# Moving the prompt's spectral product and one output gating from VectorE to GpSimd in a hybrid HGRN2 / Hyena step

## What is computed

```python
def _long_conv(u, kern):
    uf = jnp.fft.rfft(u, n=2 * L, axis=1)
    kf = jnp.fft.rfft(kern, n=2 * L, axis=0)
    return jnp.fft.irfft(uf * kf[None], n=2 * L, axis=1)[:, :L]

# _mixer
u = x1 * v
z = _long_conv(u, kern) + hy_d * u
y_hy = x2 * z
y_hy = y_hy * lax.rsqrt(jnp.mean(y_hy * y_hy, axis=-1, keepdims=True) + EPS) * hy_norm_w
merged = jnp.concatenate([o_hg, y_hy], axis=-1)
out = jnp.einsum('ble,ed->bld', merged, w_out)

# _layer
x = x + g1 * mix
```

## Time and profile before

| | us |
|---|---|
| median of 3 runs (lowest to highest) | 913.55 (912.89 to 916.66) |
| the profiled execution, its own time | 912.88 |
| its span (what the trace shows) | 911.1 |
| TensorE busy (share of the span) | 887.6 (97%) |
| VectorE busy | 717.0 (79%) |
| ScalarE busy | 443.3 (49%) |
| GpSimd busy | 38.9 (4%) |

### The profile page before, as it was taken

The page is one execution under the profiler, slowest core; times in us unless marked ns, Lnnn a source line. Parts: engine busy times, 40 slices in busy tenths (PEclk is TensorE's granted clock), DMA queues, the critical chain, the costliest instruction groups (busy, mean ns, idle before and its releaser), DMA issues.

```text
span 911.1 us, 14075 instructions
## 1 busy us (share of the span) xinstructions
PE 887.6 (97%) x5374; PEld 788.7 (87%) x5374; DVE 717.0 (79%) x911; ACT 443.3 (49%) x710; POOL 38.9 (4%) x58
## 2 busy tenths in 40 slices
PE   7999999999999999999899999999999999999997
PEld 4479898898898898688779999999999999998885
DVE  5744755966966985699678899999999999988645
ACT  5745324334343323332276756556565656565443
POOL 2200000100000000002000000000000000000000
PEclk9999999999999999999999999999999999999999
DMA  8765233144134244325511232233313232345703
GB/s 297 244 217 174 83 126 138 37 157 145 63 122 145 91 164 137 89 70 112 144 46 48 76 131 99 97 110 114 115 62 130 108 111 88 131 152 202 261 0 116
DMA packets 39275, 112.76 MB, mean 124 GB/s; under 512 B 4471, under 2 KB 12663, under 8 KB 38568
## 3 DMA queue, kind: packets, MB, share of 16 engines
q1 hardware_dynamic: 33944, 93.58, 30.3%
q0 software_dynamic: 4800, 17.99, 6.5%
q10 hardware_dynamic: 464, 0.30, 0.1%
HBM read 101.48 MB, written 10.37 MB: 123 GB/s over the span
## 4 chain that ended last, share of the span: by engine, by line
PE 84%; DVE 9%; ACT 3%; issue 2%; DMA 1%; ACTq 0%; DVEq 0%; POOLq 0%
PE ps L2005 19%; PE ps L2006 19%; PE ps L2007 19%; PE ps L2505 14%; PE ps L2226 4%; PE ps L2025 2%; PE ps L2086 2%; PE ps L2238 1%; PE ps L2363 1%; DMA part<-in_rates 1%; DVE w_lo L1377 1%; PE ps L2033 1%; PE ps L2246 1%; DMA w<-in_hy_w 1%; ACT xn L1154 1%
## 5 line engine op out<-in xcount | busy, mean ns | idle before, releaser
L2005 PE MATMUL ps<-h_hi,w_hi 128*128 128x320 f32 x620 | 196.3, 317 | 2.8 <-DVE w_lo L1377 1.4
L2007 PE MATMUL ps<-h_hi,w_lo 128*128 128x320 f32 x620 | 191.6, 309 | 0.0
L2006 PE MATMUL ps<-h_lo,w_hi 128*128 128x320 f32 x620 | 191.5, 309 | 0.0
L2005 PEld LDWEIGHTS ps<-h_hi,w_hi 128*128 128x128 f32 x620 | 116.6, 188 | 4.1 <-issue 3.1
L2006 PEld LDWEIGHTS ps<-h_lo,w_hi 128*128 128x128 f32 x620 | 116.6, 188 | 0.0
L2007 PEld LDWEIGHTS ps<-h_hi,w_lo 128*128 128x128 f32 x620 | 116.4, 188 | 0.0
L1868 DVE TENSOR_TENSOR w_lo<-raw,w_hi 128x1024 fp32r<-128x1024 f32 (+1 forms) x53 | 64.2, 1212 | 18.6 <-ACT w_hi L1220 17.6
L1220 ACT ACTIVATE w_hi<-raw 128x1024 fp32r<-128x1024 f32 (+1 forms) x53 | 55.5, 1047 | 31.8 <-PE ps L2007 31.7
L1377 DVE TENSOR_TENSOR w_lo<-raw,w_hi 128x1024 fp32r<-128x1024 f32 x44 | 53.4, 1224 | 6.4 <-ACT w_hi L904 5.2
L2005 PE MATMUL ps<-w_hi,h_hi 128*128 128x512 f32 x120 | 49.6, 413 | 2.0 <-DVE h_lo L1734 2.0
L904 ACT ACTIVATE w_hi<-raw 128x1024 fp32r<-128x1024 f32 x44 | 45.8, 1057 | 4.4 <-DMA raw<-in_slots 2.4
(11 more groups left out here) (320 smaller groups left out, 2067.2 us busy)
## 6 DMA issues: line engine op xcount, KB each, us to landing
raw<-in_slots SPq DMA_DIRECT2D x138, 512.0 KB, 4.7
acts<-actf POOLq DMA_DIRECT2D x22, 320.0 KB, 2.5
raw<-in_slots SPq DMA_DIRECT2D x24, 256.0 KB, 6.5
xf<-acts SPq DMA_DIRECT2D x12, 320.0 KB, 6.6
wsum<-acts SPq DMA_DIRECT2D x10, 320.0 KB, 7.7
xin<-in_x_sample SPq DMA_DIRECT2D x4, 512.0 KB, 11.2
grow<-gates POOLq DMA_DIRECT2D x2, 1024.0 KB, 12.3
x<-in_x_sample POOLq DMA_DIRECT2D x2, 1024.0 KB, 13.7
```

What stands on the lines that cost most here:

```text
L2005: mm(out, lhs[0], rhs[0], start=first, stop=False)
L2006: mm(out, lhs[0], rhs[1], start=False, stop=False)
L2007: return mm(out, lhs[1], rhs[0], start=False, stop=last)
```

## The change

GpSimd takes over two pieces of VectorE's work. The prompt's spectral product becomes seven instructions on GpSimd, linked to each other, behind `up_ready`; their scratch tiles are now `sq` and `x1[:, 1, NT - 1, :]` in place of `prod`, and the last one raises a new semaphore, `up_multiplied`. The gating becomes ten GpSimd instructions of 128x512, one for each tile, each behind its own `raw_taken`. VectorE's `gate_raw` and its product are gone. ScalarE's copy of the tenth tile waits for `up_multiplied`, since that tile's place is scratch until then, and TensorE's `z_prompt(0)` waits for it too. The other edits give several semaphores of the kernel's first part one shared name (`silu_in` and `bound_in` become `exp_in`, and so on) with the counts adapted, and move VectorE's wait for `ld_gate1` to before `mix_tile`.

```diff
@@ gpsimd @@
+            eng.wait_ge(sem("up_ready"), 1)
+            r, t = sq[:, 0:HW], x1[:, 1, NT - 1, :]
+            G = nc.gpsimd.tensor_tensor
+            link(G(r, Up[:, 0, :], kspec_p[:, 0, :], ALU.mult))
+            link(G(t, Up[:, 1, :], kspec_p[:, 1, :], ALU.mult))
+            link(G(r, r, t, ALU.subtract))
+            link(G(t, Up[:, 0, :], kspec_p[:, 1, :], ALU.mult))
+            link(G(Up[:, 1, :], Up[:, 1, :], kspec_p[:, 0, :], ALU.mult))
+            link(G(Up[:, 1, :], Up[:, 1, :], t, ALU.add))
+            link(nc.gpsimd.tensor_copy(Up[:, 0, :], r), "up_multiplied")
+
+            eng.wait_ge(sem("ld_gate1"), 16)
             for n in range(2):
                 cols = slice(n * HW, (n + 1) * HW)
-                eng.wait_ge(sem("raw_gated"), n + 1)
+                for i in range(NT):
+                    eng.wait_ge(sem("raw_taken"), n * NT + i + 1)
+                    x = x1[:, n, i, :]
+                    nc.gpsimd.tensor_tensor(x, x, grow1[:, int(i == NT - 1), cols], ALU.mult).then_inc(sem("raw_gated"), 1)
+                eng.wait_ge(sem("raw_gated"), (n + 1) * NT)
...
-            eng.wait_ge(sem("zspec_ready"), 3)
+            eng.wait_ge(sem("zspec_ready"), 2)
             load(grow2[:, :, :], gates[1].partition_broadcast(P), "ld_gate2")
@@ scalar @@
             for n in range(2):
                 for i in range(NT):
                     eng.wait_ge(sem("hg_mixed"), n * NT + i + 1)
+                    if n * NT + i == 2 * NT - 1:
+                        eng.wait_ge(sem("up_multiplied"), 1)
                     A(x1[:, n, i, :], ps[:, HG_BANKS[(n * NT + i) % 2], :], ACT.Copy).then_inc(sem("raw_taken"), 1)
@@ vector @@
             multiply(0)
             multiply(1)
-            eng.wait_ge(sem("up_ready"), 1)
-            r, t = prod[:, 0, 0, :], prod[:, 1, 0, :]
-            link(V.tensor_tensor(r, Up[:, 0, :], kspec_p[:, 0, :], ALU.mult))
...
-            link(V.tensor_copy(Up[:, 0, :], r), "zspec_ready")
-            def gate_raw(n):
...
-            eng.wait_ge(sem("ld_gate1"), 16)
-            gate_raw(0)
             for k in range(2):
                 split_lo(UNIT_WOUT + 4 + k)
-            gate_raw(1)
```

More of the change, by code:

```diff
@@ L813, in store_state @@
                 load(io["new_state"][0, 0].rearrange("d h k w -> h k d w")[h], newst[:, :, :], "state_stored")
+            link = linker(eng, "pool_own")
             def gate_out(which):
@@ L828, in _ @@
             eng.wait_ge(sem("raw_in0"), 32)
-            load(ktab[:, :, :, :, :], io["ktab"], "ld_ktab")
-            load(ptab_k[:, :, :], io["ptab"][:, 0], "ld_ktab")
+            load(ktab[:, :, :, :, :], io["ktab"], "filter_dma")
+            load(ptab_k[:, :, :], io["ptab"][:, 0], "filter_dma")
             def first_row(n):
@@ L837, in first_row @@
                 eng.wait_ge(sem("taps_ready"), n + 1)
-                nc.gpsimd.tensor_tensor(forth, forth, back, ALU.add).then_inc(sem("first_sum"), 1)
-                eng.wait_ge(sem("first_sum"), 1 + n // 4)
+                link(nc.gpsimd.tensor_tensor(forth, forth, back, ALU.add))
                 nc.gpsimd.tensor_copy(back, forth).then_inc(sem("first_row"), 1)
@@ L864, in _ @@
             eng.wait_ge(sem("head_steps"), HEADS * STEPS)
-            load(ptab[:, :, :, :], io["ptab"][:, 1:3], "ld_ptab")
+            load(ptab[:, :, :, :], io["ptab"][:, 1:3], "spectra_dma")
             gate_out(1)
@@ L951, in _ @@
             eng.wait_ge(sem("ld_vec"), 16)
-            eng.wait_ge(sem("silu_in"), 1)
-            A(gate_c, gate_c, ACT.Exp).then_inc(sem("silu_exp"), 1)
+            eng.wait_ge(sem("exp_in"), 1)
+            A(gate_c, gate_c, ACT.Exp).then_inc(sem("exp_done"), 1)
             eng.wait_ge(sem("ld_rates"), 16)
@@ L959, in _ @@
                   bias=rates[:, bias:bias + 1]).then_inc(sem("decay_ready"), 1)
-            eng.wait_ge(sem("bound_in"), 1)
-            A(bound[:, 1, :], bound[:, 0, :], ACT.Exp).then_inc(sem("bound_exp"), 1)
+            eng.wait_ge(sem("exp_in"), 2)
+            A(bound[:, 1, :], bound[:, 0, :], ACT.Exp).then_inc(sem("exp_done"), 1)
             A(stat[:, 2, 0, 0:1], eps[:, :], ACT.Sqrt)
@@ L1415, in _ @@
                     link(V.tensor_scalar(fr, fr, 0.5 / math.pi, None, ALU.mult))
-                eng.wait_ge(sem("hid_made"), i + 1)
+                eng.wait_ge(sem("filter_made"), i + 1)
                 if i:
@@ L1427, in _ @@
             eng.wait_ge(sem("ld_vec"), 16)
-            link(V.tensor_scalar(gate_c, v("c", 0, 2 * KD), -1.0, 80.0, ALU.mult, ALU.min), "silu_in")
+            link(V.tensor_scalar(gate_c, v("c", 0, 2 * KD), -1.0, 80.0, ALU.mult, ALU.min), "exp_in")
             lb = v("lb_f", 0, 2 * NC)
-            link(V.tensor_tensor(bound[:, 0, :], lb, lb, ALU.subtract), "bound_in")
+            link(V.tensor_tensor(bound[:, 0, :], lb, lb, ALU.subtract), "exp_in")
             def sum_groups(e):
@@ L1462, in damp @@
                 eng.wait_ge(sem("decay_ready"), n + 1)
-                eng.wait_ge(sem("taps_made"), n + 1)
+                eng.wait_ge(sem("filter_made"), n + 3)
                 b = tap_banks(n)
@@ L1493, in join @@
                 link(V.tensor_tensor(kspec[:, m, 1, cs, :], first, second, ALU.subtract), "kspec_ready")
-            eng.wait_ge(sem("silu_exp"), 1)
+            eng.wait_ge(sem("exp_done"), 1)
             link(V.tensor_scalar(gate_c, gate_c, 1.0, None, ALU.add))
@@ L1508, in _ @@
             join(0)
-            eng.wait_ge(sem("bound_exp"), 1)
+            eng.wait_ge(sem("exp_done"), 2)
             link(V.reciprocal(bound[:, 2, :], bound[:, 1, :]))
@@ L2049, in tap_pair @@
                         if d:
-                            last.then_inc(sem("taps_made"), 1)
+                            last.then_inc(sem("filter_made"), 1)
             def tap_prompt():
@@ L2109, in _ @@
             mm(ps[0:NHID, 0, 0:SIDE], w1[0:NEMB, :], feats[0:NEMB, 0:SIDE], start=True, stop=True)
-            mm(ps[NHID:P, 0, 0:SIDE], w1[0:NEMB, :], feats[0:NEMB, SIDE:2 * SIDE], start=True, stop=True).then_inc(sem("hid_made"), 1)
+            mm(ps[NHID:P, 0, 0:SIDE], w1[0:NEMB, :], feats[0:NEMB, SIDE:2 * SIDE], start=True, stop=True).then_inc(sem("filter_made"), 1)
             keep_busy(4)
@@ L2115, in _ @@
                 last = mm(ps[rows, 0, 0:SIDE], w2[rows, :], hid[rows, 0, :], start=True, stop=True)
-            last.then_inc(sem("hid_made"), 1)
+            last.then_inc(sem("filter_made"), 1)
             keep_busy(4)
@@ L2128, in _ @@
             ada_turn(0)
-            eng.wait_ge(sem("ld_ktab"), 32)
+            eng.wait_ge(sem("filter_dma"), 32)
             filter_dft(0)
@@ L2366, in _ @@
             eng.wait_ge(sem("uspec_ready"), 1)
-            eng.wait_ge(sem("ld_ptab"), 16)
+            eng.wait_ge(sem("spectra_dma"), 16)
             for cs in range(2):
```

## The result

The changed kernel is slower: 928.22 us median of 4 runs (927.26 to 929.67), against 914.25 us before (912.89 to 916.66, 4 runs). The ratio is 1.0151, with a 95% interval of 1.0124 to 1.0179. The forecast was 926.7 us. The profiled execution of the change took 929.67 us, its slowest, and has a span of 927.9 us.

The account below looks back on a forecast made before the run. The chain of waits was taken to bound the kernel, TensorE holding 84%, VectorE 9%. A 13.1 us TensorE wait and 1.8 us of clock start the loop over `c` 13.8 us later: 912.9 + 13.8 = 926.7 us, range 916 to 932.

Parts of the forecast that it names:

- The bound of the gain: At VectorE's loop over `c`: it can start no earlier than `z_ready` allows, so at most 1.1 us of 10.9 is gained.
- strict turns: Beside VectorE's `multiply` calls: GpSimd and VectorE alternate at their shared port, ending `multiply(1)` 17.3 us later; chance 0.60.
- Starving: Rival: VectorE's next instruction always gets in first, GpSimd finishes late, `mix_tile(0)` waits for a DMA; 919 to 921 us, chance 0.17.
- Cheap hand-over: Rival: GpSimd holds the port only partly, below 0.25 us delay each, so TensorE never waits; 911.8 us, chance 0.10.
- Some turns only: Rival: GpSimd gets in at every second chance, VectorE loses eight to ten turns; 918 to 920 us, chance 0.10.
- The hold of one instruction: Beside `multiply`: each GpSimd TENSOR_TENSOR delays VectorE by about 1.05 us, the COPY by 0.46 us.
- the sum: `multiply(1)` 17.3 us later less 4.2 us cover gives TensorE a 13.1 us wait; the loop over `c` starts 13.8 us later.
- The clock: At TensorE's inverse transforms after its wait: some 3.5 us at half speed, adding 1.8 us.
- From the loop to the end: Behind the loop over `c`: norm and FFN follow in one chain, so its 13.8 us shift reaches the end.
- The two new waits cost nothing: ScalarE's tenth copy and TensorE's `z_prompt(0)` wait for a product done near 398.1 undisturbed, with 17 us of cover.

Follow-up runs that it names:

- e5: The changed kernel with all seventeen GpSimd instructions, semaphores and waits kept, but on 32 of 512 columns; 913.03 us, ratio 0.9993 to before.
- e8: The changed kernel with the ten GpSimd gatings replaced by copies of a tile onto itself; 922.91 us, ratio 1.0087 to before.
- e7: The changed kernel with all four residual DMAs issued behind the tenth gating instead of two in the middle; 927.67 us, ratio 1.0148 to before.
- e9: The changed kernel with 62 filling matmuls on TensorE ahead of its wait for the latent products; 927.78 us, ratio 1.0153 to before.
- e3: The changed kernel with GpSimd's gating held back until VectorE has finished the latent products; 925.63 us, ratio 1.0130 to before.
- e6: The changed kernel with 52 filling matmuls on TensorE ahead of its wait for the latent products; 930.13 us, ratio 1.0175 to before.
- e2: The changed kernel with the prompt's product back on VectorE, gating alone on GpSimd, ScalarE's new wait gone; 921.89 us, ratio 1.0091 to before.
- e1: The changed kernel with the gating back on VectorE, the prompt's product alone on GpSimd; 915.79 us, ratio 1.0032 to before.

## Why the prediction was right, point by point

- **The bound of the gain** (1.1 us, set by `z_ready`) was right: 1.09 us in e5.
- **The mechanism** was right: strict turns between GpSimd's instructions and VectorE's with two SBUF inputs. The doubled products in the change show it, and the dose in e5, e8 and the change. The rule of the exclusive lock in the Trainium skill (SBUF — State Buffer, section "SBUF: two separate sides") agrees with these runs in the main: in e5 a 32-column GpSimd instruction waits out a VectorE product (1185 ns in all). Its "for the whole instruction" doesn't fit the measured hold, which was 0.98 of GpSimd's 1.28 us; and the product that five gatings kept out, one after the other, goes beyond what that rule would give.
- **Starving** fell: VectorE was delayed from the first turn on, and `mix_tile(0)` waited for no DMA. **Cheap hand-over** fell: 0.98 us per instruction against the 0.25 us at which it would decide. **Some turns only** fell: every product beside GpSimd's work gave a turn, until the long hold, where GpSimd got five in a row.
- **The hold of one instruction** was 0.98 us and not 1.05, and the COPY's 0.29 and not 0.46. Sixteen and one make 16.0 us, where I had 17.3; e7, which has these turns and nothing else, has 15.9 (`multiply(1)` ends 38.79 us behind the spectrum copy instead of 22.88).
- **What the sum did not have** is the product held through five gatings. It brings the delay of `multiply(1)` from 15.9 to 18.65 us (five turns would have cost 4.9 us, the hold cost 7.5). So TensorE's wait was 14.4 to 14.6 us and not 13.1.
- **The clock** was 2.28 us in the transforms and not 1.8: the low level lasted about 4.4 us of work after the wait, and not 3.5. e9 agrees with 2.04 us at the loop. It is no fixed price: behind waits of 2.06 to 14.42 us the first two transforms took 1.7 to 3.1 us longer, and not in the order of the waits, and in e3 0.1 us.
- **From the loop to the end** I carried the shift through unchanged. It lost 1.67 us on the way, as the second dip of the clock moved. At the loop the shift was 15.76 us against 13.8 forecast, and only with this loss does it come to 14.09 at `mix_tile(0)`. That the total is so near (926.7 us against a median of 928.22, 14.0 us over before) is in part luck: a turn that I had too large, a hold and a clock that I had too small, and a dip that moved nearly cancel.
- **The two new waits cost nothing**, as said: ScalarE's tenth copy began at 418.21 right behind its matmuls, and the product was done at 406.95.
- The limit of the evidence: that each turn is decided per instruction comes from the lockstep of the two timelines. No kernel here took VectorE's two-input instructions away while GpSimd worked at the same place; that PSUM inputs keep VectorE free is shown only by the rows of before.

## What to carry to other kernels

Before moving work from VectorE to an idle GpSimd, look at what VectorE runs at that moment: beside instructions with two inputs in the on-chip memory, most of the moved work's time is paid for by VectorE (0.98 of 1.28 us here), wherever in its critical stretch it falls. Here that is more than VectorE saves: it did such a 128x512 product itself in 0.69 us. Look also for a short instruction of one engine that took several times its usual duration somewhere in the trace; one such row, 0.70 us instead of 0.166, carried this forecast. And ask first what the freed engine would wait for next: of 10.9 us taken off VectorE, 1.1 us were ever to be had.

## What the runs showed that was not expected

- Behind two DMA issues from GpSimd, followed by unlinked gatings, one VectorE instruction took 8.70 us in the change (8.84 in e6, 8.88 in e9), 7.37 us in e3 and 4.92 us in e2, and with copies in place of the gatings 2.72 us (e8). With linked gatings it was 4.11 us, and without the DMA issues in between there was no such hold (e7). Why the DMA issues bring it about stays open. In the change the product started at 417.10 and must have been held almost from there, as it ended 1.1 us after the last gating (424.70), although the first gating behind the DMAs is recorded as starting only at 417.69.
- DMA issues without work behind them held nothing: in the change the two from 425.01 on ran beside products of 1.23 us. Nor did those of e5, where a product that began at 405.48, just at an issue, took 1.23 us; but only one 32-column gating followed at once there, so e5 is no test of several.
- Filling a 14.4 us wait of TensorE with matmuls up to the last 2.73 us didn't keep the clock up; up to the last 0.50 us did. A wait of 2.06 us without filling brought it down in e1, one of 2.07 us in e3 didn't. What makes the difference, no run here shows.
